# Retention stage: two stores issued later and one operand load moved ahead of a weight load

## What is computed

```
q = rotary(q, pos);  k = rotary(k, pos) * RET_DQK ** -0.5
scores = einsum('bnihd,bnjhd->bnhij', qc, kc) * intra_decay
intra  = einsum('bnhij,bnjhe->bnihe', scores, vc)
state  = state * chunk_decay + kv_n            # from chunk to chunk
cross  = einsum('bnihd,ih,nbhde->bnihe', qc, q_from_start, s_prev)
ret    = silu(g_r) * group_norm(intra + cross)
```

## Time and profile before

| | us |
|---|---|
| median of 3 runs | 1704.49 |
| lowest and highest of them | 1702.32, 1706.66 |
| the profiled execution, its own time | 1702.23 |
| its span, first to last instruction | 1700.4 |
| mean granted TensorE clock | 0.994 of full speed |
| TensorE busy | 1655.3 (97% of the span) |

### The profile page before, as it was taken

The page is one execution under the profiler, slowest core; times in us unless marked ns, Lnnn a source line. Parts: engine busy times, 40 slices in busy tenths (PEclk is TensorE's granted clock), DMA queues, the critical chain, the costliest instruction groups (busy, mean ns, idle before and its releaser), DMA issues.

```text
span 1700.4 us, 25213 instructions
## 1 busy us (share of the span) xinstructions
PE 1655.3 (97%) x9680; PEld 1375.6 (81%) x9680; DVE 1048.7 (62%) x1350; ACT 661.6 (39%) x1130; POOL 753.5 (44%) x311
## 2 busy tenths in 40 slices
PE   5999999999998999999999999999999999999998
PEld 5887877777888898988888998787888888888876
DVE  6788788778346474942121557699664738383736
ACT  5566666210223243321001256435343444435352
POOL 2011111245534353523344752572767585858550
PEclk9999999999999999999999999999999999999999
DMA  9012121275835353423111444636684665748272
GB/s 355 21 70 81 41 85 65 93 280 194 337 125 213 137 188 114 152 100 149 50 49 49 162 166 157 222 137 231 244 330 172 272 239 217 285 166 341 99 293 99
DMA packets 62709, 288.32 MB, mean 170 GB/s; under 512 B 7956, under 2 KB 8852, under 8 KB 51992
## 3 DMA queue, kind: packets, MB, share of 16 engines
q1 hardware_dynamic: 50576, 258.57, 40.6%
q10 hardware_dynamic: 12040, 28.47, 4.6%
HBM read 249.25 MB, written 37.77 MB: 169 GB/s over the span
## 4 chain that ended last, share of the span: by engine, by line
PE 80%; DVE 9%; ACT 3%; issue 3%; DMA 3%; POOL 1%; SPq 0%; ACTq 0%; POOLq 0%; DVEq 0%
PE ps L872 8%; PE ps L874 8%; PE ps L873 7%; PE ps L1282 6%; PE ps L1284 6%; PE ps L1283 6%; PE ps L1327 4%; PE ps L1326 4%; PE ps L1325 4%; PE ps L958 4%; PE ps L959 4%; PE ps L960 4%; PE ps L1162 2%; PE ps L1011 2%; DVE fs_f L2388 2%
## 5 line engine op out<-in xcount | busy, mean ns | idle before, releaser
L1282 PE MATMUL ps<-w_hi,f_hi 128*128 128x512 f32 x440 | 175.3, 398 | 3.0 <-issue 2.7
L1284 PE MATMUL ps<-w_hi,f_lo 128*128 128x512 f32 x440 | 175.1, 398 | 0.0
L1283 PE MATMUL ps<-w_lo,f_hi 128*128 128x512 f32 x440 | 174.9, 397 | 0.0
L637 POOL TENSOR_TENSOR w_hi<-raw,zero 128x1024 fp32r<-128x1024 f32 x34 | 69.1, 2031 | 228.4 <-PE ps L874 113.4
L650 POOL TENSOR_TENSOR w_lo<-raw,w_hi 128x1024 fp32r<-128x1024 f32 x16 | 41.7, 2616 | 228.8 <-ACT w_hi L1405 202.1
L725 POOL TENSOR_TENSOR w_lo<-w,w_hi 128x1024 fp32r<-128x1024 f32 x34 | 84.7, 2496 | 112.2 <-ACT w_hi L1813 65.1
L1327 PE MATMUL ps<-ring,w_hi 128*128 128x512 f32 x336 | 134.0, 399 | 0.0
L1326 PE MATMUL ps<-ring,w_lo 128*128 128x512 f32 x336 | 132.4, 394 | 0.0
L1325 PE MATMUL ps<-ring,w_hi 128*128 128x512 f32 x336 | 131.8, 392 | 0.0
L2079 DVE TENSOR_TENSOR_SCAN uu<-uu 128x512 f32<-128x512 f32 (+7 forms) x96 | 100.0, 1083 | 37.5 <-ACT uu L1498 37.5
L667 POOL TENSOR_TENSOR w_lo<-raw,w_hi 128x1024 fp32r<-128x1024 f32 x24 | 59.7, 2492 | 132.6 <-ACT w_hi L1552 131.8
(11 more groups left out here) (300 smaller groups left out, 4801.4 us busy)
## 6 DMA issues: line engine op xcount, KB each, us to landing
ring<-ops SPq DMA_DIRECT2D x42, 2048.0 KB, 8.3
raw<-wstream SPq DMA_DIRECT2D x104, 512.0 KB, 3.5
ada_r<-ada_rows SPq DMA_DIRECT2D x32, 512.0 KB, 4.5
r_lo<-aops SPq DMA_DIRECT2D x16, 1024.0 KB, 5.3
r_hi<-aops SPq DMA_DIRECT2D x16, 1024.0 KB, 7.5
w<-wstream SPq DMA_DIRECT2D x32, 512.0 KB, 3.4
aops<-as_r ACTq DMA_DIRECT2D x16, 512.0 KB, 3.5
ada_s<-ada SPq DMA_DIRECT2D x7, 1024.0 KB, 16.8
```

The source lines that it names most:

```text
L1282: nc.tensor.matmul(bank, fh, wh, start=start, stop=False, skip_group_check=skip)
L1283: nc.tensor.matmul(bank, fh, wl, start=False, stop=False, skip_group_check=skip)
L1284: return nc.tensor.matmul(bank, fl, wh, start=False, stop=stop, skip_group_check=skip)
```

## The change

Three pieces of code move; no instruction is added or removed.

1. In group 1, the store of two chunks of r is issued behind BGB's load and no longer ahead of B22's.
2. In every group, S4's load is issued ahead of BGA's load and no longer behind it.
3. The store of m1's second half is issued by ScalarE behind the high part of BGB in group 0 and no longer behind the first two high parts.

```
                 sums_load(g, 1, gemm_done, tl + 4)
+                ret_load(1, g, B22, r_wsum, 4 * g + 4)
+                sums_load(g, 3, gemm_done, tl + 8)
+                ret_load(0, g, BGA, r_wlo, 9 * g + 5)
+                ret_load(1, g, BGB, r_wlo, 9 * g + 7)
                 if g == 1:
                     sp.wait_ge(r_lo_done, 4)
                     for part, r in enumerate((r_hi, r_lo)):
                         sp.dma_start(rsave[:, part, :, :], r[:, 0:2, :].bitcast(f32)).then_inc(rs_out, 16)
-                ret_load(1, g, B22, r_wsum, 4 * g + 4)
-                ret_load(0, g, BGA, r_wlo, 9 * g + 5)
-                sums_load(g, 3, gemm_done, tl + 8)
-                ret_load(1, g, BGB, r_wlo, 9 * g + 7)
...
                 ret_high(s3, raw[:, 0, :], (r_wsum, 4 * g + 2))
                 if g == 0:
-                    act.wait_ge(ev_dve, 8 * GATE_G)
-                    act.dma_start(m1_dram[:, 4:8, :], m1s[:, 4:8, :]).then_inc(m1_out, 16)
                     act.wait_ge(mods_out, 16 * 4)
...
                 ret_high(s3, raw[:, 1, :], (ret_raw[1], 16 * (5 * g + 5)), (gemm_done, tl + 10))
+                if g == 0:
+                    act.wait_ge(ev_dve, 8 * GATE_G)
+                    act.dma_start(m1_dram[:, 4:8, :], m1s[:, 4:8, :]).then_inc(m1_out, 16)
                 for i in range(T):
                     act.wait_ge(qk_tr, 8 * g + i + 1)
```

## The result

The changed kernel takes 1708.37 us, median of 20 runs (1703.33 to 1717.05), beside 1703.9 us for the kernel before on the same chip. The ratio is 1.0028, with a 95% interval of 1.0020 to 1.0036: some 4.8 us slower, just inside the 0.3% within which the prediction calls a change no change. The forecast, 1711.0 us or 6.5 us more than before, was 0.15% too long. The profiled execution takes 1707.35 us, its span is 1705.6.

The account below looks back on a forecast made before the run. TensorE, working through 97% of the span, was taken to bound the kernel. A cost of 21.0 us for S4 ahead of BGA less 14.55 won by the two moved stores gave 6.5 us longer, 1711.0 us, range 1706 to 1715.5.

Parts of the forecast that it names:

- What bounds the kernel: TensorE works through 97% of the span; only its waits, 8.9 us for copies of v, or lower clock can be won.
- parts 1 and 3: Ahead of products 3 and 4, groups 0 and 1: moving both stores wins 9.24 + 5.3 = 14.55 us, at least 7.3.
- two signs of the prediction: In group 1, B22 lands within 6.5 us and product 4 no longer waits for it.
- Part 2, the mechanism: Every group: BGA lands 9.4 us behind S4's issue, delays ScalarE's qk copies; GpSimd's low parts hold a rotation 2.2 us.
- Part 2, the sizes: Ahead of the first gate step: waits of 3.4 us per group, 13.6 in all, plus 8.0 of clock; 21.0 net.
- the clock: Behind the wait ahead of each group's first gate step: 2.0 us lost to the lower clock, 8.0 in all.
- Rival (a): Gate steps: the 3.4 us waits come but the clock does not fall behind them; 1703.0 us, chance 0.15.
- The sum: Whole kernel: 21.0 lost less 14.55 won, 6.5 us longer, 1711.0 us.
- The two terms: At the gate steps: 13.0 us of added waits and 8.0 us of lower clock behind them.
- (b): BGA lands within 6.0 us of S4's issue, so no gate step waits; 1689.4 us, chance 0.12.
- (c): VectorE slips between GpSimd's two low parts: gate-step waits of 1.2 us each, clock up; 1694.1 us, chance 0.07.
- (d): B22 still late or m1's store slows group 1's loads: a 3.6 us wait returns; 1714.6 us, chance 0.11.

Follow-up runs that it names:

- part 1 alone: Only group 1's store of r moved behind BGB's load, on the kernel before: 1695.54 us, ratio 0.9961.
- part 3 alone: Only the store of m1's second half moved behind BGB's high part in group 0, on the kernel before: 1698.59 us, ratio 0.9975.
- parts 1 and 3 alone: The changed kernel with S4's load again behind BGA's, both stores staying late: 1691.46 us, ratio 0.9926 against the kernel before.
- copies first: The changed kernel with ScalarE's two copies of product 4 ahead of BGA's high part: 1695.66 us, ratio 0.9960 against the kernel before.

## Why the prediction was right, point by point

- **What bounds the kernel, and parts 1 and 3.** Right. The gains at the named places are 14.1 us, of 14.55. B22 in group 1 lands 7.0 us after its issue, later than the 5.6 taken and the 6.5 allowed; it is issued 2.5 us ahead of product 3 and not the 2.0 taken, and so a wait of 0.39 is left of the 6.94. Taken by the word, two signs of the prediction failed here, B22 within 6.5 us and no wait of product 4 for it; all but 0.39 of that wait went all the same. In group 0, S1's second transfer needs 13.9 us (18.7 in the earlier trace rows), and the gaps ahead of products 3 and 4 are gone. Both stores were hidden, as argued: part 1 alone and part 3 alone win without a new wait behind them.
- **Part 2, the mechanism.** Right, link by link. BGA lands 9.3, 9.7, 9.1 and 9.8 us behind S4's issue (9.4 taken). In group 2, first addition to qk to the next: 635.88 to 640.78, 4.9 us (5.2 taken, with the collision); from there to the addition that frees TensorE 3.0 (3.0). Taking out either ScalarE's order or GpSimd's second low part removes over half of the waits, both remove all.
- **Part 2, the sizes.** The waits are 11.4 us against 13.6, near 2.9 each and not 3.4. The term that was mis-sized most is the clock: 4.8 us against 8.0. I took 2.0 behind each wait from two examples; it was 1.6 behind three and nothing behind one, although 2.45 lies above the 1.94 behind which the clock had fallen. Rival (a) thus holds for one group of four.
- **The sum.** The two terms too large by 4.3 us (13.0 + 8.0 against 16.7), the gain too large by 0.5, and 1.5 of small losses that the sum did not have (0.55 at product 1, 0.9 elsewhere): 6.5 - 4.3 + 0.5 + 1.5 = 4.2, which the profile shows as 4.1; the medians give 4.8. That the forecast came so near is in part luck: the unforeseen losses and the smaller gain took back 2.0 of the 4.3 us, and single executions differ by more than that (the 20 lie between 1703 and 1717).
- **Rivals.** (b), BGA in time, and (c), short waits, are refuted by the landings and by the waits of 2.45 to 3.37; (d), a short gain, by the waits ahead of product 4, of which 0.6 us is left.

## What to carry to other kernels

A load moved ahead of another on a queue that works in order makes the other late twice: it now stands behind the moved load's own wait (5.7 us here), and then behind its bytes (3.7 us here). Before moving it, look at what the late one's consumer holds up in its engine's order, here two short copies that had nothing to do with it. Parts of a change that meet on one path do not add up: a removed wait uncovers one that stood in its shade, so cost each part with the others in place, and run them apart, which here gives a version 0.7% faster than before (parts 1 and 3 alone). Where a late transfer cannot be helped, reordering its consumer (copies first) and keeping GpSimd out of VectorE's short critical run took its whole price away.

## What was not expected of the hardware

**The clock does not go by the length of the gap alone.** Among TensorE's gaps of 1.9 to 3.4 us in retention it fell behind 1.94, 1.96, 2.02, 2.61, 2.84, 3.00, 3.02, 3.04 and twice 3.37 us, and stayed up behind 1.97, 1.99, 2.30, 2.45, 3.00 and 3.40, all kernels of this case taken together; behind the three of 5.99 to 6.94 it always fell. Even the same place differs: the windows behind the wait ahead of product 1 of group 0 show 1.00 behind a wait of 3.40 (parts 1 and 3) and 0.50 behind 2.84 (part 3 alone):

```profile
440.60:444.00 3.40, 3.40 (x29) 3.40 (x30) 0.00 (x0) 0.00 (x0) 2.19 (x1) 1.00 0.86 355
```

```profile
440.80:444.00 3.20, 3.20 (x15) 3.20 (x16) 0.00 (x0) 0.00 (x0) 2.00 (x1) 0.50 1.02 431
```

So the cost of such a wait is better taken as a chance than as a fixed sum: here it was paid ten times in sixteen. What decides it stays open. The rule that the prediction weighed, from the Trainium skill, "TensorE: Matmul & The Clock Gate", section "HAM oscillation — how this bites in real kernels", that a gap that is long enough is paid again with a slow start, holds for the three longest here. Between 1.9 and 3.4 us these runs show no length that parts the gaps that were paid from those that were not.

**A transfer that keeps its place varies.** S2's wait ahead of product 1 in group 0 was 0.15 us before, 0.69 after, and 0.88 to 3.40 in the nine experiments; its second transfer lands 7.4 to 10.6 us after its issue. It moves a single execution by up to 3 us, which blurs the parts of a few us. Its cause was not tried: the three kernels with the m1 store in its old place have 0.15, 1.74 and 1.80, the eight with it moved 0.69 to 3.40, and one profiled execution of each does not tell whether the store plays a part. The row for product 1 in the table above is thus not shown to come from the change.

**The collision is nearly an exclusive one.** VectorE's product of two SBUF operands took 2.59 us in place of 0.69 beside GpSimd's low part of 2.4. VectorE's two additions to vr at 634.25, with one operand in TensorE's banks (ps), took 1.50 us beside the first low part, the same as the two at 643.77 with GpSimd idle. The Trainium skill, "SBUF — State Buffer", section "SBUF: two separate sides", says that such an operation and a GpSimd operation that reads SBUF lock each other out for a whole instruction; the rows agree.
